# A two-block transformer kernel: sums of weight blocks made ahead in DRAM, two buffers for their parts, and 34 seven-product units in place of 26

## What is computed

```python
def sqrelu_mlp(hn, w1, w2):            # first block: hidden width 4096
    u = hn @ w1.astype(hn.dtype)
    u = jnp.square(jax.nn.relu(u))
    return u @ w2.astype(hn.dtype)
...
def swiglu(h, w_in, w_out):            # second block, twice
    gate, up = jnp.split(h @ w_in, 2, axis=-1)
    return (jax.nn.silu(gate) * up) @ w_out
```

## Time and profile before

| | |
|---|---|
| median of 3 runs | 2059.39 us (2058.56 to 2064.13) |
| the profiled execution | 2055.45 us, its span 2053.5 us, mean granted clock 0.981 |
| PE busy | 1970.8 us, 96% of the span |
| DVE, ACT, POOL busy | 1226.9, 806.8, 432.2 us |
| DMA | 175.06 MB, mean 85 GB/s |

### The profile page before, as it was taken

One profiled execution on the slowest core, in us unless ns is written; L12 is line 12 of the kernel. 1 busy time (PEld: TensorE's weight loads), 2 busy tenths in 40 slices (PEclk: granted clock), 3 DMA queues, 4 the chain that ended last, 5 costly groups with the idle time before them and its releaser, 6 DMA issues.

```text
span 2053.5 us, 29329 instructions
## 1 busy us (share of the span) xinstructions
PE 1970.8 (96%) x11954; PEld 1717.1 (84%) x11954; DVE 1226.9 (60%) x1633; ACT 806.8 (39%) x1069; POOL 432.2 (21%) x312
## 2 busy tenths in 40 slices
PE   8999989999999999999999999999997899999996
PEld 6788766788888888999899999998884578888895
DVE  6668756656565654122566566556897557566565
ACT  4448734533232433223353232234434444233232
POOL 2012230202113220013222121212245122032122
PEclk9999999999999998999999999999998999999998
DMA  4223111123232221211123233223131022223231
GB/s 176 103 83 115 62 62 62 62 103 103 86 103 100 91 95 42 82 42 42 62 83 103 83 103 104 83 103 103 62 106 40 22 83 102 103 83 103 99 106 62
DMA packets 27850, 175.06 MB, mean 85 GB/s; under 512 B 4409, under 2 KB 4537, under 8 KB 7762
## 3 DMA queue, kind: packets, MB, share of 16 engines
q1 hardware_dynamic: 25680, 167.32, 23.6%
q0 software_dynamic: 1888, 5.90, 0.9%
q10 hardware_dynamic: 162, 0.10, 0.0%
HBM read 171.19 MB, written 4.78 MB: 86 GB/s over the span
## 4 chain that ended last, share of the span: by engine, by line
PE 72%; issue 12%; DVE 6%; POOL 4%; ACT 4%; DMA 2%; SPq 0%; POOLq 0%; DVEq 0%; ACTq 0%
PE lin L533 50%; PE lin L1833 6%; PE aux L1833 5%; POOL squares L752 2%; DMA w_raw<-in_weights 1%; PE aux L1425 1%; ACT w_hi L442 1%; PE aux L2645 1%; PE lin L1627 1%; PE lin L1380 1%; DVE w_lo L449 1%; PE lin L2615 1%; POOL w_lo L449 1%; PE aux L2629 1%; POOL r_t L2245 1%
## 5 line engine op out<-in xcount | busy, mean ns | idle before, releaser
L533 PE MATMUL lin<-x_hi,w_hi 128*128 128x512 f32 (+1 forms) x1160 | 408.8, 352 | 14.5 <-DVE tmp L628 6.5
L533 PE MATMUL lin<-x_hi,w_lo 128*128 128x512 f32 (+1 forms) x1160 | 407.0, 351 | 0.0
L533 PE MATMUL lin<-x_lo,w_hi 128*128 128x512 f32 (+1 forms) x1160 | 406.8, 351 | 0.0
L449 DVE TENSOR_TENSOR w_lo<-w_raw,w_hi 128x2048 fp32r<-128x2048 f32 (+1 forms) x118 | 276.3, 2341 | 176.4 <-ACT w_hi L442 175.6
L533 PE MATMUL lin<-v_hi,w_hi 128*128 128x264 f32 (+1 forms) x1088 | 365.3, 336 | 9.0 <-DVE tmp L1873 4.1
L533 PE MATMUL lin<-v_hi,w_lo 128*128 128x264 f32 (+1 forms) x1088 | 361.3, 332 | 0.0
L533 PE MATMUL lin<-v_lo,w_hi 128*128 128x264 f32 (+1 forms) x1088 | 360.9, 332 | 0.0
L442 ACT ACTIVATE w_hi<-w_raw 128x2048 fp32r<-128x2048 f32 (+1 forms) x129 | 242.8, 1882 | 206.2 <-PE lin L533 196.1
L533 PEld LDWEIGHTS lin<-x_hi,w_hi 128*128 128x128 f32 x1160 | 219.4, 189 | 49.5 <-DVE tmp L628 7.3
L533 PEld LDWEIGHTS lin<-x_hi,w_lo 128*128 128x128 f32 x1160 | 219.7, 189 | 29.9
L533 PEld LDWEIGHTS lin<-x_lo,w_hi 128*128 128x128 f32 x1160 | 219.5, 189 | 30.0 <-issue 0.2
(11 more groups left out here) (449 smaller groups left out, 3937.7 us busy)
## 6 DMA issues: line engine op xcount, KB each, us to landing
w_raw<-in_weights SPq DMA_DIRECT2D x155, 1024.0 KB, 4.8
rel_by_distance<-rel_by_distance POOLq DMA_DIRECT2D x1, 2599.5 KB, 20.3
rel_bias<-rel_by_distance POOLq DMA_DIRECT2D x8, 264.0 KB, 3.0
h<-in_x_t SPq DMA_DIRECT2D x4, 512.0 KB, 7.7
out_t<-h SPq DMA_DIRECT2D x4, 512.0 KB, 2.8
o_t<-in_mem_t POOLq DMA_DIRECT2D x1, 1024.0 KB, 4.9
...
```

What stands on the lines that cost most here:

```text
L449: does.tensor_tensor(w_lo[:, s, 0:n], w_raw[:, s, 0:n], w_hi[:, s, 0:n].bitcast(F32), ALU.subtract).then_inc(sem("w_lo_ready"), 1)
L533: last = nc.tensor.matmul(o, a, b, start=(k % (L.kc // k_banks) == 0 and p == 0), stop=((k + 1) % (L.kc // k_banks) == 0 and p == 2))
```

## The change

There are now 34 quads: positions 3, 4, 6, 7 in `upNa`, 1, 2, 3, 5, 6, 7 in `upNb` and 1, 2, 4, 5 in `upNc`, so that quads stand in pairs and threes; the first block's six stay where they were. POOL's arithmetic on `w_raw` is gone. In its place POOL issues DMAs that copy the quads' weights into a new DRAM tensor `w_sums` and add blocks there while copying (`accum_op`), in four steps per MLP: base, pairs, triples, fours. SP loads a quad in three pieces, of which two come from `w_sums`. `ws_hi` and `ws_lo` have two buffers, and the scratch for POOL's DMA descriptors is cut to 4096 bytes. DVE and ACT get the code for a quad that follows a quad.

```diff
 QUADS = {"ff1b": (1, 3), "ff1c": (1, 3), "ff1d": (1, 3),
-         **{f"up{n}{part}": at for n in range(2) for part, at in zip("abc", ((3, 5, 7), (1, 3, 5, 7), (1, 3, 5)))}}
+         **{f"up{n}{part}": at for n in range(2)
+            for part, at in zip("abc", ((3, 4, 6, 7), (1, 2, 3, 5, 6, 7), (1, 2, 4, 5)))}}
...
-        ws_hi = sb("ws_hi", [P, 3 * BLOCK_W], F32R, scope=quad_scope)
-        ws_lo = sb("ws_lo", [P, 3 * BLOCK_W], F32R, scope=quad_scope)
+        ws_hi = sb("ws_hi", [P, 2, 3 * BLOCK_W], F32R, scope=quad_scope)
+        ws_lo = sb("ws_lo", [P, 2, 3 * BLOCK_W], F32R, scope=quad_scope)
...
+        def pool_quad_base(pool, group, *parts):
+            for run in SUM_RUNS[group]:
+                if run[0][3] in parts:
+                    pool.dma_start(quad_rows(run, w_sums, 0, 4), quad_rows(run, weights, 0, 4))\
+                        .then_inc(sem("sum_base"), 16)
+
+        def pool_quad_pairs(pool, group):
+            pool.wait_ge(sem("sum_base"), sums_made(group))
+            for run in SUM_RUNS[group]:
+                pool.dma_start(quad_rows(run, w_sums, 3, 4), quad_rows(run, weights, 0, 1), accum_op=ALU.add)\
+                    .then_inc(sem("sum_pair"), 16)
+                pool.dma_start(quad_rows(run, w_sums, 0, 1), quad_rows(run, weights, 1, 2), accum_op=ALU.add)\
+                    .then_inc(sem("sum_pair"), 16)
+
+        def pool_quad_triples(pool, group):
+            pool.wait_ge(sem("sum_pair"), 2 * sums_made(group))
+            for run in SUM_RUNS[group]:
+                pool.dma_start(quad_rows(run, w_sums, 1, 2), quad_rows(run, w_sums, 3, 4), accum_op=ALU.add)\
+                    .then_inc(sem("sum_s2"), 16)
+
+        def pool_quad_fours(pool, group):
+            pool.wait_ge(sem("sum_s2"), sums_made(group))
...
+            for run in SUM_RUNS[group]:
+                pool.dma_start(quad_rows(run, w_sums, 2, 3), quad_rows(run, w_sums, 1, 2), accum_op=ALU.add)\
+                    .then_inc(sem("sum_s4"), 16)
+
+        def sp_unit(sp, unit):
...
+            if unit > 1:
+                sp.wait_ge(sem("w_lo_ready"), unit - 1)
...
+            sp.dma_start(w_raw[:, s, BLOCK_W:], weights[unit][:, BLOCK_W:]).then_inc(sem(f"w_loaded{s}"), 16)
+            sp.wait_ge(sem("sum_pair"), 2 * made)
+            sp.dma_start(w_raw[:, s, 0:BLOCK_W], w_sums[q][:, 3 * BLOCK_W:]).then_inc(sem(f"quad_s1_{s}"), 16)
+            if q:
+                sp.wait_ge(sem("w_lo_ready"), quad_units[q - 1] + 1)
+            sp.wait_ge(sem("sum_s4"), made)
+            sp.dma_start(w_sum[:, :], w_sums[q][:, 0:3 * BLOCK_W]).then_inc(sem("quad_sums"), 16)
...
                     dve_quad_second_row(dve, L, t).then_inc(sem(f"lin_taken{slot}"), 1)
                     dve.wait_ge(sem(f"lin_taken{slot}"), before + 1)
+                    next_quad_lo(dve, L, t, 2, 3)
                     continue
...
                 def u_ready(k, up=up):
+                    k = k + 1 if k in up.quads and k + 1 in up.quads else k
...
             next_splits_after(pool, GR)
             dve_splits(pool, GR, nc.gpsimd)
+            pool_quad_fours(pool, "up0")
             pool_gates(pool)
             pool_squares(pool, l_ffn0, l_ffn0.idx)
-            pool_quad_sums(pool, "up0a", "up0b", "up0c")
+            pool_quad_base(pool, "up1", *"abc")
             pool_squares(pool, l_mix1, l_mix1.idx)
+            pool_quad_pairs(pool, "up1")
 
             next_splits_after(pool, C_)
             dve_splits(pool, C_, nc.gpsimd)
             dve_splits(pool, AQ, nc.gpsimd)
+            pool_quad_triples(pool, "up1")
             pool_latent_lo(pool)
             for L in (DK, DV):
                 dve_splits(pool, L, nc.gpsimd)
+            pool_quad_fours(pool, "up1")
             pool_attend(pool)
```

More of the change, by code:

```diff
@@ L352, in build, with runs_of @@
         quad_seq = {u: q for q, u in enumerate(quad_units)}
+        quad_layer = {L.unit0 + u: L.name for L in layer.values() for u in L.quads}
+        def runs_of(at):
+            if len({b - a for a, b in zip(at, at[1:])}) < 2:
+                return [at]
+            cuts = [0] + [x + 1 for x in range(len(at) - 1) if at[x + 1] > at[x] + 1] + [len(at)]
+            return [at[a:b] for a, b in zip(cuts, cuts[1:])]
+        SUM_RUNS = {group: [(name, run) for name in QUADS if name[0:3] == group for run in runs_of(QUADS[name])]
+                    for group in ("ff1", "up0", "up1")}
@@ L372, in pool_quad_sums, with quad_rows @@
-        def pool_quad_sums(pool, *names):
-            for name in names:
-                for t in layer[name].quads:
-                    for step in range(4):
-                        quad_sum(pool, layer[name].unit0 + t, step)
+        def quad_rows(run, t, a, b):
+            units = [layer[run[0]].unit0 + u for u in run[1]]
+            if t is w_sums:
+                t = t[quad_seq[units[0]]:quad_seq[units[-1]] + 1]
+            else:
+                t = t[units[0]:units[-1] + 1:units[1] - units[0] if len(units) > 1 else 1]
+            return t[:, :, a * BLOCK_W:b * BLOCK_W].rearrange("q p n -> p q n")
@@ L1968, in quad_low @@
                 dve.wait_ge(sem("u_lo"), base + 2 * t + 2)
-                nc.vector.engine_nop().then_inc(sem(f"lin_taken{L.tile(t % 2, 1, t // 2)[0]}"), 1)
+                if t + 1 not in L.quads:
+                    nc.vector.engine_nop().then_inc(sem(f"lin_taken{L.tile(t % 2, 1, t // 2)[0]}"), 1)
             for t in range(L.units):
@@ L2886, in _ @@
             sp.dma_start(h[:, :, 0:META], meta_t).then_inc(sem("meta_loaded"), 16)
[L2887 to L2893 removed]
+            for unit in range(2, n_units):
+                sp_unit(sp, unit)
             for t in range(0, KD, 2):
```

122 lines of the change are left out of this document (69 added, 53 removed).

## The result

The changed kernel takes 2134.32 us (median of 4 runs, 2127.25 to 2135.89), the kernel before beside it 2061.76: a ratio of 1.0344, 95% interval 1.0321 to 1.0367. It is 72.6 us slower where +41 was forecast, and lies 4 us beyond the range. The direction was right, the size was not. Both profiled executions are the fastest of their kernel (2127.25 and 2055.45 us), and their spans differ by 72.0 us, so the two traces can be set against each other.

The account below looks back on a forecast made before the run. PE, busy 96% of the span, was taken to bound the kernel. The terms -10.9 - 4.5 + 32 + 1.4 + 2.9 + 20.4 = +41.3 us, added to the median, gave about 2100 us, range 2076 to 2130.

Parts of the forecast that it names:

- Fewer matmuls: In both MLPs, eight more quads, four in each, replace slower plain units: -10.9 us.
- POOL's sums: Without POOL's summing, DVE's scaling is faster and PE's waits for second rows go: -4.5 us.
- The pairs: At 16 places where a quad follows a quad, PE waits for low parts, 2.0 us each: +32 us.
- The layer behind: Behind both MLPs, `dn` can wait for one more hidden tile of matmuls: +1.4 us.
- The gates: Six DMA issues ahead of the gates take 4.1 us, less a cover of 1.26: +2.9 us.
- Base copies and pairs ... cost nothing: These steps lie beside layers with low DMA share, costing nothing unless a quad's load outlasts its cover.
- The sparse attention: POOL's issues delay `c_lo`, and bias loads queue behind the fours, so `seen_bias` starts later: +20.4 us.
- T: Time for one step's 3.67 MB to land in DRAM: taken as 20 us, between 11.5 and 28.7.
- The bias loads do wait behind the fours: Rival in the sparse attention: bias loads are served beside the fours, delay only 6.8 us, 2087 us; chance 0.20.
- the adding steps are not as slow as 57 us: Rival in the sparse attention: adding DMAs are slow, T of 57 us, total 2173 us; chance 0.12.
- DVE does hold PE: First rival, at the pairs: DVE does not hold PE, the 32 us vanish, 2060 us; chance 0.05.
- The fourth: Rival in the MLPs: up1's base copies hold up the quads' loads, up to 18 us more, 2118; chance 0.08.

Follow-up runs that it names:

- e12_gla34: e6_all with up1's four DMA steps issued ahead of the gated attention instead of beside up0: 2050.17 us, ratio 0.9947.
- e8_q26moved: The changed kernel with the earlier kernel's 26 quads, none adjacent, and POOL's DMA steps moved as in e9_moved: 2056.18 us, ratio 0.997.
- e14_best40: e12_gla34 with 40 quads, 8192 bytes of descriptor scratch and up1's fours behind the gates: 2038.4 us, ratio 0.9879.
- e5_fill: The changed kernel plus 16 unread matmuls at each of the 16 pairs, keeping PE busy during the stall: 2116.2 us, ratio 1.0269.
- e4_order: The changed kernel with DVE making the two low parts ahead of the second row in a pair: 2089.26 us, ratio 1.0135.
- e2_pairs: The changed kernel with up1's pair DMAs issued right behind its base copies: 2127.29 us, ratio 1.0315.
- e10_scratch: The changed kernel with 8192 instead of 4096 bytes of scratch for POOL's DMA descriptors: 2125.62 us, ratio 1.0319.
- e3_late: The changed kernel with up1's triples and fours issued behind the sparse attention instead of inside it: 2108.12 us, ratio 1.0249.
- e6_all: The changed kernel, 34 quads, with DMA steps moved as in e9_moved and DVE's order as in e4_order: 2051.6 us, ratio 0.9959.
- e9_moved: The changed kernel with each MLP's four DMA steps issued together, behind the squares of an earlier MLP: 2103.39 us, ratio 1.0203.

## Why the prediction was wrong

- **Fewer matmuls, -10.9.** Not measured alone. e12_gla34 against e8_q26moved, which have up1's steps at different places, gives 6 us for eight quads, and e14_best40, with a roomier scratch too, 12 more for another six: 18 us in all for 14, where the same prices a quad give 19.
- **POOL's sums, -4.5.** Right: e8_q26moved gained 6 (4 to 9 by its interval).
- **The pairs, +32.** The stall was right to 0.1 us (2.02 from start to start), 29.4 us in all less 0.8. The step that failed is the sentence behind it, "The clock should stay at 1.00: a stop of 2 us in 12 is short". No row was given for it, and the trace of the kernel before had a stop of 1.87 us with a clock of 0.70 behind it. The clock fell behind ten of the 16 stops, at 1.5 us each, and e5_fill puts the loss at 15.5 to 18 us, about 1 us a pair. A pair costs 2.7 to 2.8 us (e4_order), not 2.0. This is the largest part of the 31 us that the sum is short.
- **The layer behind, +1.4.** Right or a little high: PE's waits for the low hidden tile are 2.0 and 1.2 us in two each, against 0.6.
- **The gates, +2.9.** Mis-sized: measured +7.3. The issues were 4.3 us, but the next product took 2.7 us longer behind them; 7.0 us and not 4.1 was the term, above my bound of 6.8. Less the cover of 1.3 that is 5.7; the rest came in DVE's operations beside POOL's products, which had no term.
- **"Base copies and pairs ... cost nothing".** Failed at the index scores, +8.3. I looked for cost in the DMA share and not in POOL's own program: the pairs stand ahead of a weight split, and the scratch, cut to 4096 bytes by the same change, holds six of these. e2_pairs and e10_scratch each take the wait away. The diff had the line; I gave it no term.
- **The sparse attention, +20.4.** Right in mechanism and near in size, +22.5: T 22.4 instead of 20 (where the 20 was luck, as said above), and POOL 6.1 us late instead of 2.7. PE felt less than the sum of both (at `seen_bias` it is 1598.76 - 1540.93 - 31.6 = 26.2 us).
- **The rivals.** The bias loads do wait behind the fours (e3_late), the adding steps are not as slow as 57 us, and DVE does hold PE. The fourth, copies beside quads, is true but small at 34 quads (0.7 us at one pair, the 2.0 us of e6_all) and 12 us at 40.

The range was too short for the reason that also missed the centre: it had bounds for each term that I had written down, and none for a term that I had not.

What stays open: why the clock falls behind some of these stops and not behind others of the same length (8 to 11 of 16 in six executions with the same pairs); and why the sparse attention ran at clocks of 0.87 to 0.95 in different kernels, which moves the time by some us and holds the 6 us between e9_moved and its expectation.
